# A split-precision two-block decoder kernel: the last modulation group is made beside the MLP's first quarter, the other seven one place earlier

## The reference

```python
cond = jax.nn.silu(c)
mod = cond @ mod_w[i] + mod_b[i]                     # 2048 -> 12288
sh1, sc1, g1, sh2, sc2, g2 = jnp.split(mod, 6, axis=-1)
h = _rms_norm(x, norm1_g[i]) * (1.0 + sc1) + sh1
y = _conv_mixer(h, ...)        # 2048 -> 4096, GLU, 31-tap depthwise conv, LayerNorm, silu, 2048 -> 2048
x = x + (1.0 + g1) * y
h = _rms_norm(x, norm2_g[i]) * (1.0 + sc2) + sh2
u = jnp.square(jax.nn.relu(h @ mlp_w1[i]))           # 2048 -> 8192
x = x + (1.0 + g2) * (u @ mlp_w2[i])                 # 8192 -> 2048
```

## Time and profile before

| what | value |
|---|---|
| time, median of 3 runs | 2604.83 us (2601.93 to 2605.74) |
| profiled execution: its time | 2605.78 us |
| profiled execution: span of the core | 2604.1 us |
| TensorE busy | 2552.5 us, 98% |
| VectorE busy | 1877.0 us, 72% |
| ScalarE busy | 1290.4 us, 50% |
| data moved | 553.16 MB, mean 212 GB/s |

### The profile page before, as it was taken

One profiled execution on the slowest core, in us unless ns is written; L12 is line 12 of the kernel. 1 busy time (PEld: TensorE's weight loads), 2 busy tenths in 40 slices (PEclk: granted clock), 3 DMA queues, 4 the chain that ended last, 5 costly groups with the idle time before them and its releaser, 6 DMA issues.

```text
span 2604.1 us, 38960 instructions
## 1 busy us (share of the span) xinstructions
PE 2552.5 (98%) x14522; PEld 2186.4 (84%) x14522; DVE 1877.0 (72%) x2098; ACT 1290.4 (50%) x1695; POOL 231.5 (9%) x270
## 2 busy tenths in 40 slices
PE   8999999999999999999999999999999999999999
PEld 7888888888877888887888879997788888888887
DVE  6796658878878768887678756989566565565564
ACT  5645545544444446553455456687544344343443
POOL 2000000010010000000000004772000000000000
PEclk9999999999999999999999999999999999999999
DMA  6643447899999765778777744543556666666655
GB/s 206 175 131 107 141 119 258 300 334 315 320 346 324 259 220 175 251 267 273 261 244 252 254 146 154 167 157 116 175 179 191 191 184 193 183 187 196 192 187 168
DMA packets 291491, 553.16 MB, mean 212 GB/s; under 512 B 17121, under 2 KB 96018, under 8 KB 290578
## 3 DMA queue, kind: packets, MB, share of 16 engines
q1 hardware_dynamic: 270994, 442.06, 53.0%
q0 software_dynamic: 18720, 102.77, 11.7%
q10 hardware_dynamic: 1632, 6.29, 0.6%
HBM read 548.96 MB, written 2.10 MB: 212 GB/s over the span
## 4 chain that ended last, share of the span: by engine, by line
PE 79%; DVE 8%; DMA 6%; ACT 4%; issue 3%; POOL 0%; SPq 0%; POOLq 0%; DVEq 0%; ACTq 0%
PE sums L668 30%; PE small L668 10%; PE small L701 9%; PE sums L701 9%; DMA mod_raw<-in_mod_w_dram 5%; PE small L703 5%; PE sums L703 5%; PE sums L720 4%; DVE w_lo L622 2%; PE sums L722 2%; DVE mod_acc L1454 2%; ACT w_hi L613 1%; PE small L1808 1%; DMA raw<-in_w_in_dram 1%; PE sums L1500 0%
## 5 line engine op out<-in xcount | busy, mean ns | idle before, releaser
L613 ACT ACTIVATE w_hi<-raw 128x1024 fp32r<-128x1024 f32 x814 | 859.7, 1060 | 1165.9 <-PE sums L668 350.1
L622 DVE TENSOR_TENSOR w_lo<-raw,w_hi 128x1024 fp32r<-128x1024 f32 x814 | 1004.2, 1242 | 577.2 <-ACT w_hi L613 574.7
L701 PE MATMUL sums<-x_two,w_hi 128*128 128x512 f32 x1024 | 363.7, 399 | 2.6 <-DVE x_two L1050 1.9
L701 PE MATMUL small<-x_two,w_hi 128*128 128x512 f32 x1024 | 361.2, 397 | 0.0
L703 PE MATMUL sums<-x_two,w_lo 128*128 128x256 f32 x1024 | 288.1, 281 | 0.0
L703 PE MATMUL small<-x_two,w_lo 128*128 128x256 f32 x1024 | 287.4, 281 | 0.0
L668 PE MATMUL sums<-w_hi,x_two 128*128 128x512 f32 x896 | 281.6, 392 | 0.0
L668 PE MATMUL sums<-w_hi,y_hi 128*128 128x512 f32 x672 | 264.7, 394 | 7.8 <-DVE gate L2762 3.4
L668 PE MATMUL sums<-w_hi,y_lo 128*128 128x512 f32 x672 | 262.3, 390 | 0.0
L668 PE MATMUL sums<-w_lo,y_hi 128*128 128x512 f32 x672 | 262.2, 390 | 0.0
L1454 DVE SCALAR_TENSOR_TENSOR mod_acc<-mod_raw,cond,mod_acc 128x1536 f32<-128x1536 f32 x120 | 217.7, 1814 | 57.5 <-DMA mod_raw<-in_mod_w_dram 57.2
(11 more groups left out here) (437 smaller groups left out, 3957.9 us busy)
## 6 DMA issues: line engine op xcount, KB each, us to landing
raw<-in_mlp_w_dram SPq DMA_DIRECT2D x256, 512.0 KB, 4.3
raw<-in_w_in_dram SPq DMA_DIRECT2D x198, 512.0 KB, 4.6
mod_raw<-in_mod_w_dram POOLq DMA_DIRECT2D x128, 768.0 KB, 6.6
raw<-in_w_up_dram SPq DMA_DIRECT2D x128, 512.0 KB, 4.2
raw<-in_w_down_dram SPq DMA_DIRECT2D x64, 512.0 KB, 4.8
raw<-in_conv_w_in_dram SPq DMA_DIRECT2D x128, 256.0 KB, 3.7
raw<-in_w_o_dram SPq DMA_DIRECT2D x32, 512.0 KB, 6.2
raw<-in_conv_w_out_dram SPq DMA_DIRECT2D x32, 512.0 KB, 3.8
```

Of the source, the lines that this page charges most:

```text
L613: act.activation(w_hi[:, s.slot(k), :], raw[:, s.slot(k), :], ACT.Copy).then_inc(hi_ready, 1)
L622: dve.tensor_tensor(w_lo[:, s.slot(k), :], raw[:, s.slot(k), :], w_hi[:, s.slot(k), :].bitcast(F32), ALU.subtract).then_inc(lo_ready, 1)
L701: pe.matmul(to[:, b, :], w_hi[:, s.slot(k), c], both, start=kt == 0, stop=False, skip_group_check=True)
```

## The change

Three groups instead of four are made over the four merge rounds; which chunk takes how many adds is now a table, `MOD_MERGE`, and `MOD_ENDS` names the round and chunk in which each of the three groups ends. The groups behind them slide one place earlier (group 3 in `mix_out`, 4 in `cross_q` and the FFN, 5 and 6 in the FFN). The last group, 7, is made in the first quarter of the MLP, with tiles of its own: its 16 row blocks are loaded through GpSimd's queue into `last_raw` (two buffers) once the last norm is under way; its adds stand among the low halves of the second, third and fourth up chunk (4, 6 and 6); the transposes stand on TensorE in `mlp_down`'s first chunk behind the first unit; the reduce and one wide diagonal `last_diag` follow on VectorE; the four wide products stand at tile 12 of the same chunk; ScalarE's four copies follow. `gate_act` and `gate_pe` are gone. The second gain vector (1 + sc2 times the norm's weight) is made later in the FFN, since its group is kept later. The merge loop and the first quarter's down loop are written out instead of looped.

```diff
+                last_diag = sb("last_diag", [P, KT, P], scope=s1)
+                last_raw = sb("last_raw", [P, 2, MOD_W], scope=s1)
+                last_acc = sb("last_acc", [P, MOD_W], scope=s1)
...
+        MOD_MERGE = ((3, 3, 3, 2, 1, 0), (4, 0, 4, 2, 1, 1), (4, 4, 0, 2, 1, 1), (3, 3, 3, 2, 1, 0))
+        MOD_ENDS = ((1, 1), (2, 2), (3, 5))
...
+            pool.wait_ge(nf_split, NF_SPLITS[NF_MLP] + NG)
+            for kt in range(KT):
+                if kt >= 2:
+                    pool.wait_ge(mod_used, (MOD_G - 1) * KT + kt - 1)
+                pool.dma_start(last_raw[:, kt % 2, :],
+                               mod_w_2[0][kt * P:(kt + 1) * P, (MOD_G - 1) * MOD_W:]).then_inc(mod_loaded[kt % 2], 16)
...
             beside_unit(LAST, s.size + 3)
-            gate_act(act)
             square_act(act, CV_C - 1)
...
-                for m, units in enumerate((5, 5, 4, 2, 0, 0)):
+                for m, units in enumerate(MOD_MERGE[i]):
...
+            def gains(k, name):
+                dve.wait_ge(mod_kept, 3 + 4 * k)
...
-                if j == 0:
-                    dve.wait_ge(diag_summed, 8)
...
+            def last_unit(j):
+                m = next(last_mods)
+                mod_unit(dve, m, m % KT, rows=last_raw, acc=last_acc)
+
+            def up_pair(L, i, done=0, mods=(0, 0)):
                 for m in range(2):
                     s = spot("mlp_up", m, L, (i, 16, 2))
-                    rest_units(dve, s, SLOTS + (0 if m else done), s.size + SLOTS)
+                    rest_units(dve, s, SLOTS + (0 if m else done), s.size + SLOTS, last_unit, mods[m])
...
+                    if gated and m == 0:
+                        rest_units(dve, s, first, first + 1)
+                        mod_keep(dve, own, MOD_G - 1, MOD_G)
+                        dve.wait_ge(mod_kept, MOD_G)
+                        wide_dve(dve, 5, last_diag)
+                        rest_units(dve, s, first + 1, end)
+                        dve.wait_ge(diag_kept, 8)
...
-            up_pair(L, 0, len(NF_MORE))
-            up_pair(L, 1)
+            up_pair(L, 0, len(NF_MORE), (0, 4))
+            up_pair(L, 1, 0, (6, 6))
...
-            gate_pe(pe)
...
+            def gate_first(tile, end):
+                pe.wait_ge(ml_split, tile // 4 + 1)
+                if tile == 2:
+                    added(pe, spot("mlp_up", 1, (0, MLP_U, MLP_C), (1, 16, 2)))
+                    mod_sum(pe, MOD_G * KT, acc=last_acc)
+                elif tile == 12:
+                    wide_pe(pe, 1, last_diag)
```

More of the change, by code:

```diff
@@ L2604, in _ @@
             up_pair(L, 1)
-            with act.Fori(0, 2) as i:
-                down(L, i, False)
+            for i in range(2):
+                down(L, i, False, i == 0)
             with act.Fori(1, MLP_Q - 1) as q:
@@ L2855, in mods @@
             def mods():
-                for m in range(5 * KT + MOD_CROSS, 8 * KT):
+                for m in range(4 * KT + MOD_CROSS, 7 * KT):
                     mod_unit(dve, m, m % KT)
                     yield m
+            def gains(k, name):
+                dve.wait_ge(mod_kept, 3 + 4 * k)
+                own.step(dve.scalar_tensor_tensor(out=eff[:, k, :], in0=mod[:, (1 + 3 * k) * KT:(2 + 3 * k) * KT], scalar=1.0,
+                                                  in1=parm(name, 0, KT), op0=ALU.add, op1=ALU.mult))
+                own.wait()
             ffn_mods = mods()
@@ L2903, in _ @@
                 if f == 1:
-                    dve.wait_ge(mod_kept, 7)
-                    for k, name in enumerate(("n1", "n2")):
-                        own.step(dve.scalar_tensor_tensor(out=eff[:, k, :], in0=mod[:, (1 + 3 * k) * KT:(2 + 3 * k) * KT], scalar=1.0,
-                                                          in1=parm(name, 0, KT), op0=ALU.add, op1=ALU.mult))
-                    own.wait()
+                    gains(0, "n1")
                 for c in range(4):
@@ L3085, in up, with down @@
                     up_pair(L, i)
-            def down(L, i, last):
+            def down(L, i, last, gated=False):
                 for m in range(2):
                     s = spot("mlp_down", m, L, (i, 16, 2))
-                    rest_units(dve, s, *ahead(s, last and m == 1))
+                    first, end = ahead(s, last and m == 1)
+                    if gated and m == 0:
+                        rest_units(dve, s, first, first + 1)
[4 more added lines that the diff above has]
+                        dve.wait_ge(diag_kept, 8)
+                    else:
+                        rest_units(dve, s, first, end)
                     c = nf_columns(2 * i + m)
@@ L3216, in merge @@
                     multiply(pe, spot("merge", m, L), x_hi, x_lo, False,
-                             before=merge_before(i - 1) if i and m == 0 else None, beside=beside)
+                             before=merge_before(i - 1) if i and m == 0 else sum_before(i, m), beside=beside)
                 if beside is not None:
@@ L3357, in up, with down_first @@
                     multiply_two(pe, spot("mlp_up", m, L, (i, 16, 2)), m)
+            def gate_first(tile, end):
[5 more added lines that the diff above has]
+                    wide_pe(pe, 1, last_diag)
+            def down_first(L):
+                for c in range(4):
+                    if c == 2:
+                        pe.wait_ge(diag_kept, 8)
+                    multiply(pe, spot("mlp_down", c % 2, L, (c // 2, 16, 2)), y_hi, y_lo, False, to=down_sums(c // 2, c % 2),
+                             before=gate_first if c == 0 else None)
             def down(L, q, last=False):
```

123 lines of the change are left out of this document (56 added, 67 removed).

## The result

The change is slower: 2620.43 us median of 5 runs (2615.01 to 2623.49) against 2605.74 us (2601.93 to 2611.98). The ratio is 1.0048 with a 95% interval of 1.0032 to 1.0065, so 8 to 17 us. The profiled execution took 2620.74 us, of it 2619.1 span, 15.0 us more span than before.

What follows compares the result with a forecast made beforehand. TensorE, busy 2552.5 of 2604.1 us, was taken as the bound. Terms -3.0 - 0.3 + 20 + 3.0 + 1.7 = +21.4 us on the profiled 2605.8 give 2627.2; the median, 1.0 lower, is 2626.2, range 2614 to 2635.

Steps and rivals of the forecast that it cites:

- Rival A: First MLP quarter: adds wait for rows as in cross_q, TensorE stands 14 to 27 us; the forecast itself, chance 0.65.
- rival B: First MLP quarter: rows land early, in 4 to 5 us; stop 8 to 14 us, time 2614 to 2620; chance 0.15.
- C: First MLP quarter: late low halves delay weight loads, queues slow each other; stop over 27 us, +30 to +38; chance 0.10.
- The sign that the transposes start some 20 us behind the first unit of `mlp_down`: What the profile after would show at the column sums if the forecast was right; within 2 us would mean wrong.
- part (3): First MLP quarter: 16 adds in 24 units make TensorE 21.1 us late at the sums, low-half stops included; taken as +20.
- the first reason for rival A: First MLP quarter: six rows and eight units in 22.6 us demand 394 GB/s; the merge stage moves 326.
- the twin in cross attention: The cross_q chunk, also eight low halves and six adds with row waits, from which a block was put at 27.4 us.
- The lower bound: First MLP quarter: without row waits a block is 20.8 us and TensorE is 7.9 us late at the sums.
- (1): Merge rounds: 64 modulation adds become 48, the three gate-product waits go; taken as -3.0 us, between 0 and -4.
- (4): Other work added in the MLP: gate products +3.0 us, moved transposes 0, one half-clock stretch after the stop +1.7.
- (5): Other groups slide one place earlier, second gain vector made later, loops of merge and mlp_down written out: 0.
- The end of the convolution: ScalarE's 16 gate diagonals go, second sum comes forward: -0.3 us; removing TensorE's gate matmuls gives 0, at most +1.6.

Runs made afterwards that it cites:

- Run 1: The change with four row buffers for the last group instead of two, nothing else: 2610.48 us, ratio 1.0009 to the kernel before.
- run 5: The change without the last group's loads, adds, transposes and reduce; its diagonal, gate products and copies kept, made from gate 1's part: 2599.82 us, ratio 0.9978.
- run 8: The change with its three merge groups packed into the first four chunks of each round, as before: 2623.86 us, ratio 1.0073.
- run 2: The change with only the last group's first two row blocks loaded and reused by all 16 adds, 14 loads left out: 2609.48 us, ratio 1.0010.
- run 7: The change with the last group's adds as 4, 4, 4, 4 over the up chunks, transposes left in place: 2613.57 us, ratio 1.0026.
- run 9: The change with adds 1, 4, 5, 4 and 2, four row buffers, transposes before the seventh unit, gate products in the second chunk: 2603.28 us, ratio 0.9990.
- run 10: As run 9, but with the change's two row buffers instead of four: 2604.12 us, ratio 0.9989 to the kernel before.

## Why the prediction came out as it did

**The sign, the place and the size of the stop were right.** The forecast was 2626.2 us in a range of 2614 to 2635; measured were 2620.4. Rival A's mechanism showed: VectorE idle on row loads from the seventh row on, the transposes waiting, the clock falling behind the stop. By the median alone the result is also at the upper edge of rival B (2620); the waits for rows of up to 4.41 us tell the two apart. Run 1, where rows are in time, shows what B would have been: a stop of 5.1 us, not 8 to 14. The chances of A, B and C add up to 0.90, not to the 0.89 that stands there for slower.

Two things of it were wrong beside the gain that is treated below. The sign that the transposes start some 20 us behind the first unit of `mlp_down` did not come: it was 8.7 us, because TensorE had already lost the rest at the low halves, as part (3) itself says. And the first reason for rival A, a demand of 394 GB/s against the 326 of the merge rounds, is not what made the rows late. The change moved 398 GB/s from 1919 to 1929 with TensorE busy throughout, and in run 1 the same loads were waited for nowhere. The rows were late because each was asked for late, with two buffers.

**The first MLP quarter, term by term.** In the change's own time the third block was forecast to start at 1943.7 - 9.6 = 1934.1 and started at 1934.19. The two blocks were to take 27.4 us each by the twin in cross attention and took 27.8 and 24.1, the second with shorter waits. That makes TensorE's lateness at the transposes 21.1 - 2.9 = 18.2 us; the rows give 1991.79 - 1982.99 + 9.6 = 18.4. The term of +20 was 1.6 too large. The stops at low halves (7.8 us) were inside it and not beside it, as forecast, and so were their clock stretches. Behind it came 1.3 us of transposes that had been set at 0, about 1.5 us of half clock (the transposes took 2.79 us at 1991.79; forecast +1.7), and 3.4 to 3.6 us of gate products (forecast +3.0; run 5 shows 3.59 with nothing beside). Forecast 24.7, measured 24.6, since the errors cancel. That it fits to 0.1 us is luck: run 8, with the same code in the MLP, loses 21.6 us there in its profile.

**The lower bound was set too high.** A block without row waits was put at 8 x 1.23 + 6 x 1.82 = 20.8 us. Run 1 shows 19.5: back to back, the next instruction starts before the end that the profile gives for the last, every 1.14 and 1.73 us (the pair of low halves in the earlier trace rows, 2.35 us, had shown it). Two blocks of 19.5 put the stop at 7.9 - 2.6 = 5.3 us, and runs 1 and 2 have 5.1 and 5.2.

**What was wrong is the gain ahead of the MLP: forecast 3.3 us, measured 9.6 in this pair of profiles.** The step that failed is the sum of parts (1), (4) and (5). The change, runs 1 to 7 and runs 9 and 10 have the same instructions ahead of the MLP. In their ten profiles TensorE gains 4.1 to 10.3 us on the kernel before, counted from 370 us to the end of `conv_out` (the change: 9.5). So the forecast was too small in all ten, and the 9.6 is near the upper end of what single executions show.

Two places have a gain in all ten. First, the merge rounds, where 3.0 were forecast: 4.2 to 5.9 us up to the end of the last round (the change: 4.8). Of it 1.3 us are the twelve transposes that a group takes with it when it leaves; part (4) counted them as nothing at both ends. The late starts at the gate products gave back 3.9 us in the change, a new wait ahead of the transposes of the merged rows took 1.0, and 0.6 are in small pieces. Second, the start of `ffn_down`, where nothing was forecast and no add was moved: 2.0 to 4.0 us (the change: 2.6). Windows of the kernel before and of the change around the same products:

```profile
1190.00:1205.00 15.00, 12.70 (x49) 9.99 (x48) 14.42 (x12) 5.17 (x6) 1.06 (x2) 0.89 0.72 230
```
```profile
1183.00:1198.00 15.00, 13.69 (x61) 11.02 (x60) 14.70 (x13) 4.80 (x5) 1.05 (x2) 1.00 0.71 233
```

Before, VectorE was 2.3 us late there and 0.89 of the clock was granted; in the change it was 1.3 us late and the clock stayed at 1.00. In the ten other runs it was between 0 and 2.2 us late, and always at a granted clock of 1.00. Only one execution of the kernel before was profiled, so whether the stretch belongs to that kernel or to that execution stays open.

A third piece belongs to the one execution of the change. Behind the last gate product the memory's transposes waited for VectorE in the kernel before (its waits of 480 to 830):

```profile
PE small L811 <- DVE mem_x L795: 1.1, 1, 1.1
```

In the change's profile this wait is missing, worth 1.2 us. But it is there in the profile of every run, 0.5 to 1.6 us; this is run 9's:

```profile
PE small L814 <- DVE mem_x L798: 1.2, 1, 1.2
```

**The end of the convolution** went as forecast. TensorE stands 6.21 us ahead of `conv_out` in the change, then runs at half clock (products of 0.63 us instead of 0.40 in the timeline) and falls back 1.7 us against before; the next units, which before waited for VectorE, give all of it back, and at the end of them it has gained 0.5 us where 0.3 were forecast.

**The Trainium skill** ("DMA: Bandwidth & Descriptors", "Anatomy of one DMA — SWDGE (gpsimd) path") would have had a row land in an estimated 3.8 us. In the loaded quarter it was 6.9 us, and the shortest landing, there and in the kernel before, was 4.5; the measurement decides. No run here was made to load a row with nothing else in the queues, so whether the price holds then is not shown.

## What to carry to other kernels

Work that fills an engine's idle time is hidden only as long as a whole period fits: the sum of the block (low halves, adds, relu-square) against the bound engine's period, and separately how much time the bound engine still has between the block's end and the first instruction that needs the result. Here six adds a period overran by 1.3 us a chunk and the consumer stood one unit behind; four or five adds and a consumer six units behind left a stop of 0.9 us (four buffers) or 2.1 (two). With two buffers, a load of 6.9 us and an add of 1.8 allow one row in about (6.9 + 1.8) / 2 = 4.4 us, which is an estimate; where more was asked, four buffers took the waits for rows away (run 1), and dead tiles could lend them. When work is taken out of a stage, count the instructions that it takes along on the bound engine (here 1.3 us of transposes). And read a gain of a few microseconds from several executions: here the same instructions gained 4 to 10 us.

## What the runs showed of the hardware

The stops of 2.9, 4.9 and 8.7 us in the MLP were each followed by a stretch at half clock (products of 0.63 us instead of 0.39, mean clock 0.84 and 0.90 in the windows), which I had expected once and not three times. Run 9, without such a stop, has 1.00 throughout its 72 us.

The first MLP quarter can carry more than I took for its limit: its window in run 9 moves 307 GB/s at a DMA share of 0.85 with no stop, and the change moved 344 GB/s at 0.99 in 12.5 us of it (1970.5 to 1983), against 326 at 0.93 in the merge rounds. Over 1919 to 1929 the change moved 398 GB/s. What rows lost there was the time from a late request to the landing, not the bandwidth: run 1, with four buffers, moved 333 GB/s over 1915 to 1980 and waited for no row.

Executions of the same instructions differ before any change begins: at 370 us, TensorE stands between 2.6 us behind and 2.2 us ahead of the kernel before in the eleven profiles.
